# The reciprocal roots of the eight prompt-attention tails: ScalarE's Sqrt, or a guess from the bits and Newton steps on GpSimd

## The reference, cut to what matters

```
p = softmax(q k^T * scale + alibi, causal)        # two 64-wide maps per head, 4 heads
a = p[:, 0] - lam * p[:, 1]
oa = a @ v                                        # 128 wide per head
oa = oa * rsqrt(mean(oa^2, -1) + EPS) * g_oa * (1 - lam_init)
ua = (oa * silu(az)) @ w_branch[0]
```

## Time and profile before

| | |
|---|---|
| median of 3 runs | 1376.41 us (1375.38 to 1378.98) |
| the profiled execution: its time | 1372.81 us |
| the profiled execution: its span | 1371.0 us |
| TensorE busy (matmul) | 1295.5 us, 94% of the span |
| VectorE busy | 546.8 us, 40% |
| ScalarE busy | 478.3 us, 35% |
| GpSimd busy | 108.7 us, 8% |
| stage A and the last tail | about 208 to 443 us from the start of the span |

### The profile page before, as it was taken

How to read it: one execution, slowest core, us unless ns; L and a number is a source line. 1 busy time by engine, 2 the same in 40 slices (tenths; PEclk the granted TensorE clock), 3 DMA queues, 4 the chain that set the end, 5 groups by cost and what they waited for, 6 DMA issues and landing times.

```text
span 1371.0 us, 19401 instructions
## 1 busy us (share of the span) xinstructions
PE 1295.5 (94%) x7846; PEld 1117.5 (82%) x7846; DVE 546.8 (40%) x1187; ACT 478.3 (35%) x1064; POOL 108.7 (8%) x126
## 2 busy tenths in 40 slices
PE   6999999999876999999798899999999999999998
PEld 5778778888655876788676797788999999999876
DVE  5654344556673225277723343312232222222411
ACT  5543223655674235256512343212222111221200
POOL 0010000000001000000110000000122222222000
PEclk9999999999999999999799899999999999999999
DMA  8432111111005320102212302431111131110422
GB/s 276 139 111 71 46 47 36 31 32 32 1 1 183 116 72 17 31 24 70 70 36 62 104 24 85 146 112 33 37 46 47 47 108 47 47 47 29 141 85 69
DMA packets 89930, 94.47 MB, mean 69 GB/s; under 512 B 8498, under 2 KB 64626, under 8 KB 89714
## 3 DMA queue, kind: packets, MB, share of 16 engines
q1 hardware_dynamic: 85506, 79.33, 18.9%
q0 software_dynamic: 4336, 13.90, 2.8%
HBM read 79.32 MB, written 13.89 MB: 68 GB/s over the span
## 4 chain that ended last, share of the span: by engine, by line
PE 86%; ACT 5%; DVE 5%; issue 2%; DMA 1%; SPq 0%; POOLq 0%; POOL 0%; ACTq 0%; DVEq 0%
PE heavy L835 14%; PE heavy L836 14%; PE heavy L837 14%; PE heavy L847 9%; PE heavy L849 8%; PE heavy L848 8%; PE heavy L897 4%; PE scores L947 2%; PE attended L967 1%; PE transposed L956 1%; PE scores L1203 1%; PE transposed L924 1%; PE scores L1104 1%; PE attended L1220 1%; ACT arena L1489 1%
## 5 line engine op out<-in xcount | busy, mean ns | idle before, releaser
L1362 ACT ACTIVATE arena<-heavy 128x364 f32<-128x364 f32 (+1 forms) x108 | 51.0, 473 | 370.2 <-PE heavy L837 370.2
L835 PE MATMUL heavy<-h_hi,rc_hi 128*128 128x364 f32 (+1 forms) x384 | 132.4, 345 | 2.1 <-DVE arena L2140 2.1
L836 PE MATMUL heavy<-h_lo,rc_hi 128*128 128x364 f32 (+1 forms) x384 | 128.0, 333 | 0.0
L837 PE MATMUL heavy<-h_hi,rc_lo 128*128 128x364 f32 (+1 forms) x384 | 127.9, 333 | 0.0
L835 PE MATMUL heavy<-h_hi,rp_hi 128*128 128x364 f32 (+1 forms) x384 | 126.3, 329 | 0.0
L836 PE MATMUL heavy<-h_lo,rp_hi 128*128 128x364 f32 (+1 forms) x384 | 126.1, 328 | 0.0
L837 PE MATMUL heavy<-h_hi,rp_lo 128*128 128x364 f32 (+1 forms) x384 | 126.1, 328 | 0.0
L1817 DVE SCALAR_TENSOR_TENSOR arena<-arena,heavy 128x364 f32<-128x364 f32 (+1 forms) x48 | 25.5, 532 | 213.7 <-PE heavy L837 213.7
L614 POOL TENSOR_TENSOR merged<-merged,arena 128x364 f32<-128x364 f32 (+1 forms) x48 | 67.2, 1400 | 442.4 <-DVE arena L1817 442.4
L835 PEld LDWEIGHTS heavy<-h_hi,rc_hi 128*128 128x128 f32 x384 | 74.0, 193 | 6.5 <-issue 3.1
L836 PEld LDWEIGHTS heavy<-h_lo,rc_hi 128*128 128x128 f32 x384 | 74.0, 193 | 0.0
(11 more groups left out here) (312 smaller groups left out, 2901.2 us busy)
## 6 DMA issues: line engine op xcount, KB each, us to landing
out<-arena POOLq DMA_DIRECT2D x36, 256.0 KB, 3.4
rc_whole<-w_in SPq DMA_DIRECT2D x16, 512.0 KB, 3.8
rp_whole<-w_in SPq DMA_DIRECT2D x16, 512.0 KB, 3.9
arena<-x_prompt SPq DMA_DIRECT2D x8, 512.0 KB, 5.7
arena<-cache_k_a SPq DMA_DIRECT2D x16, 256.0 KB, 3.4
arena<-cache_v_a SPq DMA_DIRECT2D x16, 256.0 KB, 3.6
ra_whole<-w_in SPq DMA_DIRECT2D x8, 512.0 KB, 4.0
arena<-cache_mem_k SPq DMA_DIRECT2D x8, 512.0 KB, 5.2
```

Source lines behind the costliest of these rows:

```text
L835: nc.tensor.matmul(out, a_hi, b_hi, start=(x == 0), stop=False)
L836: nc.tensor.matmul(out, a_hi, b_lo, start=False, stop=False)
L837: end = nc.tensor.matmul(out, a_lo, b_hi, start=False, stop=(x == len(terms) - 1))
L1362: nc.scalar.activation(tanh[m % 2][:, 0:cw], bank[:, 0:cw], ACT.Tanh, scale=0.5)\
```

## The change

ScalarE keeps the Squares of the eight prompt tails and drops their Sqrts. VectorE makes x = sum/128 + ssq and a first guess of its reciprocal root, from the bits (halved by a shift and taken from a constant): three instructions of 128x4, in step 4k+7 between `softmax_map` and `combine`. GpSimd refines it with three Newton steps of four instructions each (128x4, each waiting for the one before), twelve per tail, and gives the semaphore `oroot_done` that ScalarE gave. VectorE's reciprocal in `tail_scale` goes for these eight tails. The other tails (k >= 8) stay as they are. On GpSimd the first seven tails stand ahead of the clearing of `qpad`, the eighth behind the copies of the new keys.

```diff
@@ GpSimd
+            def tail_newton(k):
+                x, y, a = ostat[:, 0, :], ostat[:, 2, :], ohalf[:, :]
+                pool.wait_ge(guessed, k + 1)
+                for i in range(3):
+                    settle(pool.tensor_tensor(out=a, in0=y, in1=y, op=ALU.mult))
+                    settle(pool.tensor_tensor(out=a, in0=a, in1=x, op=ALU.mult))
+                    settle(pool.tensor_scalar(a, a, -0.5, 1.5, ALU.mult, ALU.add))
+                    end = pool.tensor_tensor(out=y, in0=y, in1=a, op=ALU.mult)
+                    if i < 2:
+                        settle(end)
+                end.then_inc(oroot_done, 1)
+
+            for k in range(PT - 1):
+                tail_newton(k)
...
             for x in range(2):
                 pool.tensor_copy(kTs[x][:, :, PAST:NSK], kT[:, :, NP_TOK:T]).then_inc(new_keys, 1)
                 pool.wait_ge(new_keys, x + 1)
+            tail_newton(PT - 1)
@@ ScalarE, tail_root_A
                 for h in range(H):
-                    settle(nc.scalar.activation(waste[:, :], og[:, h * P:(h + 1) * P], ACT.Square,
-                                                accum_out=ostat[:, 0, h:h + 1]))
-                for h in range(H):
-                    end = nc.scalar.activation(ostat[:, 1, h:h + 1], ostat[:, 0, h:h + 1], ACT.Sqrt,
-                                               bias=ssq[:, h:h + 1], scale=1.0 / P)
-                end.then_inc(oroot_done, 1)
+                    end = nc.scalar.activation(waste[:, :], og[:, h * P:(h + 1) * P], ACT.Square,
+                                               accum_out=ostat[:, 0, h:h + 1])
+                    if h < H - 1:
+                        settle(end)
+                end.then_inc(squares_done, 1)
+                act.wait_ge(squares_done, k + 1)
@@ VectorE
+            def tail_guess(k):
+
+                x, y = ostat[:, 0, :], ostat[:, 2, :]
+                dve.wait_ge(squares_done, k + 1)
+                settle(nc.vector.scalar_tensor_tensor(out=x, in0=x, scalar=1.0 / P, in1=ssq[:, :], op0=ALU.mult, op1=ALU.add))
+                settle(nc.vector.tensor_scalar(y.bitcast(I32), x.bitcast(I32), 1, None, ALU.logical_shift_right))
+                nc.vector.tensor_scalar(y.bitcast(I32), y.bitcast(I32), -1, 0x5F3759DF, ALU.mult, ALU.add).then_inc(guessed, 1)
+
             def tail_scale(k):
                 n = tail_rows(k)
                 dve.wait_ge(oroot_done, k + 1)
-                settle(nc.vector.reciprocal(ostat[0:n, 2, :], ostat[0:n, 1, :]))
+                if k >= PT:
+                    settle(nc.vector.reciprocal(ostat[0:n, 2, :], ostat[0:n, 1, :]))
...
                 if u in A_TAIL:
                     tail_scale(A_TAIL[u])
+                if u - 1 in A_END:
+                    tail_guess(A_END[u - 1])
...
             page_evict(0)
+            tail_guess(PT - 1)
             tail_scale(PT - 1)
```

More of the change, by code:

```diff
@@ L376, in hybrid_step @@
         rstat = sb("rstat", [P, 3])
-        ostat = sb("ostat", [P, 3, H])
+        ostat, ohalf = sb("ostat", [P, 3, H]), sb("ohalf", [P, H])
         ssum, ssq, waste = sb("ssum", [P, 2, H]), sb("ssq", [P, H]), sb("waste", [P, P])
@@ L418, in hybrid_step @@
         o_full, o_free, oroot_done = sem("o_full"), sem("o_free"), sem("oroot_done")
+        guessed, squares_done, newton = sem("guessed"), sem("squares_done"), sem("newton")
         ob_free = sem("ob_free")
@@ L557, in _, with settle @@
                         pool.dma_start(mk_kept, mk_first).then_inc(mk_out, 16)
+            steps = [0]
+            def settle(ins):
+                steps[0] += 1
+                ins.then_inc(newton, 1)
+                pool.wait_ge(newton, steps[0])
+            def tail_newton(k):
[11 more added lines that the diff above has]
+                tail_newton(k)
             pool.wait_ge(sc_read, 2 * NU)
```

## The result

| | before | after |
|---|---|---|
| median | 1376.41 us (1372.75 to 1378.98, 5 executions) | 1365.36 us (1364.61 to 1366.03, 4 executions) |
| ratio of the times | | 0.992, 95% interval 0.9901 to 0.9939 |
| profiled execution: time, span, mean granted clock | 1372.81, 1371.0, 0.981 | 1365.91, 1364.1, 0.980 |
| TensorE, VectorE busy | 1295.5, 546.8 us | 1295.9, 549.4 us |
| ScalarE, GpSimd busy | 478.3, 108.7 us | 450.4, 132.0 us |

A fifth execution of the changed kernel (1469.74 us, clock 0.839) was disturbed and is left out. The forecast was 1369.1 us, with 1365.4 to 1374.7 for the range.

What follows compares the result with a forecast made beforehand. TensorE, busy for 94% of the span, was taken as the bound. Gains of 0.3 + 0.69 + 1.94 + 2.93 + 1.63 = 7.49, less 0.2, made 7.3 us: 1369.1 us from the median, range 1365.4 to 1374.7.

Steps and rivals of the forecast that it cites:

- Tails 0 to 2: Heavy-job steps: of TensorE's 0.48 and 1.45 us idle around tails 1 and 2, 0.3 us is gained.
- Tail 3: TensorE's two waits behind it, 0.44 for ScalarE's copy and 0.25 for VectorE's softmax map, both go: 0.69 us.
- Tail 4: TensorE's two waits behind it, 1.14 and 0.80 us, both go: 1.94 us.
- Tail 5: Without a heavy job, step 27 should shrink from 8.46 us to step 28's 5.53: a gain of 2.93.
- Tail 6: Transposes behind `combine(30)` begin at 412.97 instead of 414.60, the gain cut off by VectorE's 0.60 us guess: 1.63 us.
- Contention: GpSimd's Newton steps of tails 5 and 6 beside VectorE's combining get in each other's way: 0.2 us lost.
- the last one: From profiled execution to median: 1365.5 us forecast for the former, the median 3.6 us above it, so 1369.1 us.
- (a): Only one of two loads in tails 5 and 6 was on the path: gain 5.0 us, 1371.4; chance 0.14.
- (b): GpSimd and VectorE exclude each other often in tails 5 to 7: 4.1 us less gain, 1373.2; chance 0.09.
- (c): GpSimd slow at small instructions, so tail 7 waits: costs from 0.43 us apiece, 1379.5 us at 1.3; chance 0.05.
- (d): ScalarE's lead pays more: early tails' idle time goes too, tail 6 doesn't pay the guess; 9.5 us, 1366.9; chance 0.10.
- (e): Nothing moves, since TensorE's waits have other causes and the loads were hidden: 1376.4 us; chance 0.07.

Runs made afterwards that it cites:

- the repetition: The kernel before, with no edit, profiled a second time: 1376.2 us, ratio 0.9992 to the kernel before.
- the two repetitions: Both kernels with no edit, each profiled a second time: before 1376.2 us (0.9992), after 1364.82 us (0.9902 to the kernel before).
- the version on VectorE: The changed kernel with guess and Newton steps both on VectorE, none on GpSimd: 1375.68 us, 0.9994 to the kernel before.

## Why the prediction was right and where it was not

The mechanism was right: all 16 loads go, 20.5 us of ScalarE, and TensorE gets only what the loads of the late tails cost it. Its steps:

- Tails 0 to 2, 0.3: behind tail 2 the lead of `scores` over before is 0.44. Right.
- Tail 3, 0.69: step 19 is 0.95 shorter. Tail 4, 1.94: step 23 is 2.26 shorter. Both too small: I added up the waits in the timeline, and the steps had lost more than these.
- Tail 5, 2.93: 3.10 between the two first traces, and up to 4.4 in other executions of before. The step was priced by a comparison of steps 27 and 28, and that step 27 stood at half clock for 3.4 us (0.60 and 0.55 in the windows, both within the step) was not seen. In the repetition this stretch begins 1.4 us later and reaches into step 28.
- Tail 6, 1.63: 1.85. The guess takes 0.46, not 0.60, and VectorE comes out of the softmax maps 4.79 us behind the start of `scores(31)`, not 4.87 (403.81 - 399.02; 411.06 - 406.19).
- Tail 7, nothing: right, with 2.0 us to spare where 1.6 were worked out (5.2 less 3.6).
- The reciprocals of `tail_scale`, not counted: steps 25 and 29 are each 0.21 shorter, since what VectorE does ahead of `tail_final` is on the path there.
- Contention, -0.2: nothing that reaches TensorE. GpSimd's instructions of 0.20 us take 0.57 and 0.59 beside the combining of step 31, the combining takes 1.42 as before. Of the two it is GpSimd that waits. The Trainium skill, SBUF — State Buffer, says of the shared port pair that a VectorE instruction with two SBUF inputs and a GpSimd instruction that reads SBUF exclude each other; the trace's 0.57 and 0.59 agree with it, and it shows the cost on one side only.
- GpSimd at 0.30 apiece with the wait: 0.28 where nothing disturbs it.

Up to unit 30 these differences go one way: 0.14 for tails 0 to 2, 0.2 for tail 3 (of its 0.95, 0.07 is given back a step later), 0.32, 0.17 and 0.22 for tails 4 to 6, 0.42 for the two reciprocals and 0.2 for the contention are 1.7 us, the difference between 7.3 and 9.0. The page's load moved along, as said, and its wait is 0.56 us shorter (9.5 at the page). Then 2.6 us go again, at half clock behind that wait, which neither the forecast nor a rival foresaw: 6.9 are left. The errors nearly cancel. The profiled execution was to come to 1365.5 and came to 1365.91; that it came so close is luck. How long the clock is at half behind the page wait is not fixed by the change either: with all 16 loads gone it is 10.2 us in both traces of after, and 6.8 in the runs with six Newton steps and with the guess behind the combining.

The step that failed is therefore the last one, "The median of the three runs is 3.6 us above it; taken from the median it is 1369.1 us". The 3.6 us were carried over unchanged, as if they belonged to any kernel. Measured, the median of after (1365.36) lies 0.55 us below its profiled execution (1365.91). So the profiled execution was missed by 0.4 us and the distance to the median by 4.15, and that is the miss: 6.9 us between the profiled executions and 4.15 are the 11.05 us of the medians. In the two repetitions the median lies 1.0 us above the profiled execution (before) and 5.7 us below it (after): the distance is scatter of the one execution that was profiled. The one of before was among the fastest (clock 0.981, where the mean of all is 0.978).

What this scatter consists of is known in part. It goes with the time at half clock. Every trace with Sqrt in tail 5 has a half-clock stretch between 383 and 390 us (before, its repetition, the run with tails 0 to 4 changed), and no trace without has one. At equal clock the change is worth 8.3 to 8.9 us; the 1.0 to 1.6 us beyond 7.3 are terms that were sized too small. The rest of the 11 us goes with a mean clock that is higher after (0.981 instead of 0.978). That is read from the grouping of executions by clock, not from a run that fixes it, and why the mean clock is higher stays open: the traces don't show fewer such stretches. In all they hold 53.4 and 57.7 us at half clock before, 56.8 and 70.3 after. Up to 570 us it is 17.1 in both traces of before and 20.5 and 23.9 in those of after; the rest lies behind, where the change alters nothing. And one execution of after also had 0.975 and took 1370.49.

Of the rivals, (a) is refuted by step 27 (3.10, not 1.28) and by the run with the loads alone taken away, (b) by the combining that keeps its length, (c) by 0.28 us apiece, (e) by the result. (d) comes nearest in size, 9.5 us, and by its second reason only in part: step 31 pays for the guess, but less than I took, and of the 1.9 us of the earlier trace rows only 0.44 went.

## What to carry to other kernels

Price the removal of a stall by the time from one landmark to the next, compared with a like step that has no stall, and not by the waits that name it: the step also holds what stood behind, and slow matmuls after a stall. Before adding a trace's gain to a median, look at the granted clock of several executions and of the windows behind each wait: here the wait for the page, 1.9 to 3.7 us, is followed by 3.4 to 10.2 us at half clock in all traces that have it but one, and filling two waits with a heavy job was worth 8 to 10 us more, nearly as much as the change itself. The distance between one profiled execution and the median is not a property to carry over: it was 3.6 and 1.0 us for one kernel, -0.55 and -5.7 for the other. Small dependent arithmetic belongs on whichever engine has margin: the same Newton steps cost TensorE nothing on GpSimd, and on VectorE the whole gain went.

## What the hardware showed that was not expected

- The length of a half-clock stretch does not follow that of the wait: at the page it is 3.4 us behind a wait of 3.7 us in the first trace of before, 6.8 behind the same wait in its repetition, 10.2 behind 3.12 us in after, and nothing behind 3.04 us in the run with tails 0 to 4 changed. A shorter wait can thus be followed by a larger loss, or by none.
- Small instructions on GpSimd (128x4) take 0.20 us, and 0.28 from one to the next when each waits for the one before; on VectorE they take 0.15 to 0.20, and about 0.20 from one to the next. The first shift by integers took 0.74 us in one place (step 31 of the version on VectorE), for which no cause was found.
